# Routed experts of a two-layer trunk: passes counted one by one instead of in pairs

## The reference, cut to what matters

```
s = sigmoid(t @ w_router);  idx = top 4 of (s + b_router);  w = s[idx] / sum(s[idx]) * 2.5
routed = sum over the 4 chosen e of  w_e * (silu(t @ w_e_gate[e]) * (t @ w_e_up[e])) @ w_e_down[e]
shared = (silu(t @ w_s_gate) * (t @ w_s_up)) @ w_s_down
x = x + gate2 * rmsnorm(routed + shared)
```

| layer | tokens of the largest expert of the groups, in order of rank |
|---|---|
| 0 | 176, 121, 109, 84, 69, 59, 48, 37 |
| 1 | 274, 123, 104, 77, 67, 58, 49, 27 |

## Time and profile before

### The profile page before, as it was taken

The page is one execution under the profiler, slowest core; times in us unless marked ns, Lnnn a source line. Parts: engine busy times, 40 slices in busy tenths (PEclk is TensorE's granted clock), DMA queues, the critical chain, the costliest instruction groups (busy, mean ns, idle before and its releaser), DMA issues. The chain is left out here.

```text
span 2462.8 us, 36549 instructions
## 1 busy us (share of the span) xinstructions
PE 2316.8 (94%) x13640; PEld 1420.9 (58%) x13640; DVE 1051.0 (43%) x2010; ACT 636.6 (26%) x1575; POOL 511.7 (21%) x562
## 2 busy tenths in 40 slices
PE   6999999999999999899979999999999999989996
PEld 3656554666577645555455665656656765545552
DVE  3544344643156335322466253546323733452225
ACT  2225201630033022222231350046001501312221
POOL 0213030040224100233221221203012330013331
PEclk8999999999999999999989999999999999999999
DMA  9123465101343021899651226410042312074985
GB/s 327 42 95 103 171 220 177 44 34 60 120 112 89 35 81 40 342 373 398 244 195 69 86 77 253 165 57 1 35 145 104 103 62 72 35 280 184 376 350 229
DMA packets 170192, 368.37 MB, mean 150 GB/s; under 512 B 38836, under 2 KB 52156, under 8 KB 170052
## 3 DMA queue, kind: packets, MB, share of 16 engines
q1 hardware_dynamic: 116400, 259.96, 28.7%
q10 hardware_dynamic: 29972, 56.10, 6.4%
q0 software_dynamic: 23680, 50.43, 6.1%
HBM read 343.99 MB, written 47.56 MB: 159 GB/s over the span
## 5 line engine op out<-in xcount | busy, mean ns | idle before, releaser
L2780 PE MATMUL ps<-ring,mixT 128*32 128x256 f32 x2688 | 215.7, 385 | 1.2 <-DMA ring<-in_w_e_up 1.2
L234 PE MATMUL ps<-ring,hT 128*128 128x512 f32 x480 | 210.3, 595 | 4.8 <-PEq L1401 4.1
L2780 PEld LDWEIGHTS ps<-ring,mixT 128*32 128x32 f32 x2688 | 118.1, 112 | 96.9 <-issue 22.4
L234 PEld LDWEIGHTS ps<-ring,hT 128*128 128x128 f32 x480 | 89.8, 190 | 116.0 <-issue 115.5
L1504 PE MATMUL ps<-late,ring 128*128 128x320 f32 x512 | 145.4, 443 | 3.7 <-PEq L2046 2.5
L2647 PE MATMUL ps<-ring,mixT 128*128 128x512 f32 x320 | 140.5, 598 | 4.4 <-PEq L1401 4.4
L1504 PEld LDWEIGHTS ps<-late,ring 128*128 128x128 f32 x512 | 98.8, 194 | 48.2 <-issue 9.3
L835 PE MATMUL ps<-hT,ring 128*128 128x512 f32 x256 | 114.5, 600 | 2.9 <-ACT ssm_dec L1081 2.9
L2798 PE MATMUL ps<-ring,ex_hidT 128*32 128x512 f32 x768 | 115.4, 598 | 0.7 <-DMA ring<-in_w_e_down 0.7
L412 PE MATMUL ps<-hT,ring 128*128 128x320 f32 x368 | 107.2, 444 | 4.9 <-PEq L1346 2.7
L1467 PE MATMUL ps<-mix_T,mix_S 128*128 128x320 f32 x384 | 107.2, 434 | 3.0 <-DVE mix_part L1590 1.6
(11 more groups left out here) (549 smaller groups left out, 4432.9 us busy)
## 6 DMA issues: line engine op xcount, KB each, us to landing
ring<-in_w_in SPq DMA_DIRECT2D x18, 2048.0 KB, 10.2
ring<-in_w_gate SPq DMA_DIRECT2D x12, 2048.0 KB, 9.8
da_ada_w<-in_w_ada ACTq DMA_DIRECT2D x12, 2048.0 KB, 8.7
ring<-in_w_e_down SPq DMA_DIRECT2D x48, 512.0 KB
ring<-in_w_e_gate SPq DMA_DIRECT2D x40, 512.0 KB
ring<-in_w_e_up SPq DMA_DIRECT2D x40, 512.0 KB
mix_ada_w<-in_w_ada ACTq DMA_DIRECT2D x8, 2048.0 KB, 18.0
ring<-y_rows SPq DMA_DIRECT2D x28, 512.0 KB, 7.9
```

Source lines behind the costliest of these rows:

```text
L234: last = pe.matmul(out, cx.hT[:, k, tok(t)], wide[:, k, :], start=(k == 0), stop=(k == KT - 1))
L2780: ins = pe.matmul(ps[rows, 2 + b, 0:2 * P].rearrange("p (g f) -> p g f", g=2), xT[:, b, k, rows], ew[:, :, k, :], start=(k == 0), stop=(k ...
```

## The change

A group now takes passes one by one: its count is that of its largest expert's sets of 32 tokens, rounded up, and at least 2. The total is rounded up to an even number, in the last group, since ScalarE, VectorE and GpSimd still loop over two passes at a time; TensorE loops over one. `xT`, `hid`, `hidT` and the PSUM banks of `up` (2), `turn_hidden` (3) and `down` (4, 5) are now single. A new buffer `xs` is fixed: VectorE copies the gathered rows from `xg` into it (`stage_rows`), and `turn` reads `xs`. `gather(n)` waits for the copy of pass n-2 and no longer for its transposes. TensorE's order is `up(i) down(i-1) turn(i+1) turn_hidden(i)`, with the first pass of each group written out ahead of the loop. A few VectorE steps of one column each prepare and compute the counts. The core of the diff:

```diff
 LANES = 4
 GRAIN = P // LANES
 GROUPS = NE // LANES
 STRIDE = 3
 N_CHOICE = TOP_K * TILES
...
         before = old[:, 4 * D + TOP_K * TILES * NE:4 * D + (TOP_K + 1) * TILES * NE].rearrange("p (t e) -> p t e", t=TILES)
         xg = old[:, 0:2 * D].rearrange("p (b d) -> p b d", b=2)
-        xT = old[:, 2 * D:4 * D].rearrange("p (b k s) -> p b k s", b=2, k=KT)
+        xs = old[:, 2 * D:3 * D]
+        xT = old[:, 3 * D:4 * D].rearrange("p (k s) -> p k s", k=KT)
...
-                    pool.wait_ge(sem("x_turned"), at(n - 1, i))
-                pool.tensor_copy(index[:, b:b + 1], m.table[:, bass.ds(at(n, i), 1)] if n >= 4 else m.table[:, n:n + 1]).then_inc(
+                    pool.wait_ge(sem("x_staged"), at(n - 1, j))
...
-            def turn(n, i=0):
-                b = n % 2
-                pe.wait_ge(sem(f"xg_ready{b}"), i * (16 * UNROLL // 2) + 16 * (n // 2 + 1))
-                if n:
-
-                    pe.wait_ge(sem("xT_low"), at(n, i))
-                    pe.wait_ge(sem("xT_high"), at(n, i))
+            def turn(n):
+
+                pe.wait_ge(sem("x_staged"), n + 1)
                 for k in range(KT):
-                    ins = pe.transpose(ps[:, k // 4, (k % 4) * P:(k % 4 + 1) * P], xg[:, b, k * P:(k + 1) * P],
-                                       cx.ident)
+                    ins = pe.transpose(ps[:, k // 4, (k % 4) * P:(k % 4 + 1) * P], xs[:, k * P:(k + 1) * P], cx.ident)
                 ins.then_inc(sem("x_turned"), 1)
...
             pe.wait_ge(sem("shared_hid"), 1)
             turn(0)
-            turn(1)
             pe.wait_ge(sem("experts_known"), 1)
             pe.wait_ge(sem("shared_hid"), 2)
             first = 0
             for s in range(GROUPS):
-                last = turns(pe, s)
+                last = passes(pe, s)
                 pe.wait_ge(sem(f"up_full{s % 2}"), 2 * LANES * 16 * (s // 2 + 1))
-                with pe.Fori(first, last) as i:
-                    up(0, i, s)
-                    up(1, i, s)
-                    turn_hidden(0, i)
-                    turn(2, i)
-                    pe.wait_ge(sem(f"down_full{s % 2}"), LANES * 16 * (s // 2 + 1))
-                    down(0, i, s)
-                    turn_hidden(1, i)
-                    turn(3, i)
-                    down(1, i, s)
+                up(first, s)
+                if s:
+                    down(first - 1, s - 1)
+                turn(first + 1)
+                turn_hidden(first)
+                pe.wait_ge(sem(f"down_full{s % 2}"), LANES * 16 * (s // 2 + 1))
+                with pe.Fori(first + 1, last) as i:
+                    up(i, s)
+                    down(i - 1, s)
+                    turn(i + 1)
+                    turn_hidden(i)
                 first = last
+            down(last - 1, GROUPS - 1)
...
+            def turned(n, j=0):
+                act.wait_ge(sem("x_turned"), at(n + 1, j))
+                if n:
+
+                    act.wait_ge(sem("tile_up"), at(n, j))
+                act.activation(xT[:, 0:4, :].rearrange("p k s -> p (k s)"), ps[:, 0, :], ACT.Copy).then_inc(
                     sem("xT_low"), 1)
 
...
+            count = half_passes(act)
+            silu_up(0)
+            turned(1)
+            hidden_out(0)
+            silu_up(1)
+            result(0)
+            turned(2)
+            hidden_out(1)
+            with act.Fori(1, count) as j:
+                for n in range(2):
+                    silu_up(n, j)
+                    result(n - 1, j)
+                    turned(n + 1, j)
+                    hidden_out(n, j)
+            result(-1, count)
...
-            whole(t_of, n_of, 1.0 / PER_TURN, (PER_TURN - 1.0) / (2 * PER_TURN))
-            step(dve, dve.tensor_scalar(t_of, t_of, 1.0, None, ALU.max))
+            whole(t_of, n_of, 1.0 / GRAIN, (GRAIN - 1.0) / (2 * GRAIN))
+            step(dve, dve.tensor_scalar(t_of, t_of, 2.0, None, ALU.max))
...
-            dve.tensor_reduce(ids[:, 1:2], pick[:, 0, 1, :], AX.X, ALU.add).then_inc(sem("ids_ready"), 1)
+            step(dve, dve.tensor_reduce(so_far, pick[:, 0, 1, :], AX.X, ALU.add))
+            whole(half, so_far, 0.5, 0.25)
+            step(dve, dve.tensor_scalar(half, half, of_half, None, ALU.mult))
+            dve.scalar_tensor_tensor(out=ids[:, 1:2], in0=so_far, scalar=of_sum, in1=half, op0=ALU.mult,
+                                     op1=ALU.add).then_inc(sem("ids_ready"), 1)
...
+            def stage_rows(n, j=0):
+
+                b = n % 2
+                dve.wait_ge(sem(f"xg_ready{b}"), j * 16 + 16 * (n // 2 + 1))
+                if n:
+                    dve.wait_ge(sem("x_turned"), at(n, j))
+                dve.tensor_copy(xs[:, :], xg[:, b, :]).then_inc(sem("x_staged"), 1)
+
+            def turned(n, j=0):
+                dve.wait_ge(sem("x_turned"), at(n + 1, j))
+                if n:
+                    dve.wait_ge(sem("tile_up"), at(n, j))
+                dve.tensor_copy(xT[:, 4:8, :].rearrange("p k s -> p (k s)"), ps[:, 1, :]).then_inc(
                     sem("xT_high"), 1)
 
...
             dve.wait_ge(sem("experts_known"), 1)
             turned(0)
+            stage_rows(1)
+            count = half_passes(dve)
+            hidden(0)
             turned(1)
-            count = turns(dve, GROUPS - 1)
-            with dve.Fori(0, count) as i:
-                hidden(0, i)
-                hidden(1, i)
-                turned(2, i)
-                result(0, i)
-                turned(3, i)
-                result(1, i)
+            stage_rows(2)
+            hidden(1)
+            result(0)
+            turned(2)
+            stage_rows(3)
+            with dve.Fori(1, count) as j:
+                for n in range(2):
+                    hidden(n, j)
+                    result(n - 1, j)
+                    turned(n + 1, j)
+                    stage_rows(n + 2, j)
+            result(-1, count)
```

More of the change, by code:

```diff
@@ L60 @@
 N_CHOICE = TOP_K * TILES
[L61 to L63 removed]
+MAX_PASSES = 2 * TOK // GRAIN + 2 * GROUPS
+TABLE = MAX_PASSES + 6
 EVEN = 12582912.0
@@ L2513, in stage_tail, with passes, half_passes, at @@
         block = st.enter_context(nc.Block())
[L2515 to L2521, removed]
+        def passes(eng, s):
+            return eng.value_load(m.words[0:1, P + s:P + s + 1], min_val=2 * s + 2, max_val=MAX_PASSES)
+        def half_passes(eng):
+            return eng.value_load(m.words[0:1, P + GROUPS:P + GROUPS + 1], min_val=GROUPS, max_val=MAX_PASSES // 2 + 1)
+        def at(n, j):
+            return j * 2 + n
         @block.sync
@@ L2563, in _ @@
                 if s >= 2:
-                    passed = turns(sp, s - 2)
-                    sp.wait_ge(sem("tile_up"), passed * UNROLL)
+                    passed = passes(sp, s - 2)
+                    sp.wait_ge(sem("tile_up"), passed)
                 for c in range(LANES):
@@ L2627, in _ @@
             gather(3)
[L2628 to L2633, removed]
+            with pool.Fori(0, count) as j:
+                for n in range(2):
+                    gather(n + 4, j)
+                    scatter(n, j)
+            pool.wait_ge(sem("xg_ready1"), count * 16 + 32)
+            pool.wait_ge(sem("xg_ready0"), count * 16 + 32)
             pool.sem_inc(sem("pool_go"), 1)
@@ L2932, in _ @@
             turned(0)
-            turned(1)
             act.wait_ge(sem("table_known"), 1)
@@ L2970, in _ @@
             ins.then_inc(sem("spare_rows"), 1)
+            so_far, half, of_half, of_sum = (tiny[:, n:n + 1] for n in range(4))
+            step(dve, dve.tensor_scalar(of_half, col, float(GROUPS - 1), 2.0, ALU.is_equal, ALU.mult))
+            step(dve, dve.tensor_scalar(of_sum, col, float(GROUPS), None, ALU.is_equal))
+            step(dve, dve.tensor_tensor(of_half, of_half, of_sum, ALU.add))
+            step(dve, dve.tensor_scalar(of_sum, col, float(GROUPS - 1), None, ALU.is_lt))
             finish_mods(cx, dve, 1, mods).then_inc(sem("mods_known"), 1)
@@ L3081, in _ @@
             step(dve, dve.tensor_scalar(tmp, lane, FAR, None, ALU.mult))
-            step(dve, dve.scalar_tensor_tensor(out=begin, in0=begin, scalar=float(PER_TURN), in1=tmp, op0=ALU.mult,
+            step(dve, dve.scalar_tensor_tensor(out=begin, in0=begin, scalar=float(GRAIN), in1=tmp, op0=ALU.mult,
                                                op1=ALU.add))
@@ L3152, in _, with result @@
+            dve.sem_inc(sem("y_low"), 1)
+            dve.sem_inc(sem("y_high"), 1)
+            shared(1)
+            stage_rows(0)
+            def result(n, j=0):
+                b = n % 2
+                dve.wait_ge(sem("tile_down"), at(n + 1, j))
+                dve.wait_ge(sem(f"y_stored{b}"), j * 16 + 16 * ((n + 2) // 2))
+                dve.tensor_copy(y[:, b, SEC:D], ps[:, 5, :]).then_inc(sem("y_high"), 1)
             dve.wait_ge(sem("experts_known"), 1)
             turned(0)
+            stage_rows(1)
```

116 lines of the change are left out of this document (44 added, 72 removed).

## The result

| | before | changed |
|---|---|---|
| median, us | 2465.1 (2455.6 to 2473.7, 4 runs) | 2490.8 (2481.6 to 2499.5, 4 runs) |
| ratio, first comparison | | 1.0118 (95% interval 1.0078 to 1.0158) |
| ratio, second comparison (run e12 below) | | 1.0087 (1.0059 to 1.0115) |
| profiled execution: time; span | 2464.5; 2462.8 | 2489.8; 2487.7 |
| passes in layers 0 and 1 | 28, 32 | 26, 30 |

A forecast was written before the change was run, and what follows sets the result against it. TensorE's own sequence was taken as the bound, with the DMA engines close behind. +20.2 (passes and wait) - 2 (stalls) - 0.4 (ahead of first pass) = +17.8 us, forecast 2477 us; own range 2470 to 2486, 8-in-10 range 2462 to 2495.

The forecast's parts named there:

- The counts: Expert passes of both layers: 28+32 = 60 become 26+30 = 56, four fewer at 6.44 us, -25.8 us.
- rival (e): Expert passes: the schedule gives other totals than computed, each pass 7.26 us; chance small, within the forecast's 0.63.
- The wait added: TensorE ahead of `up`: 0.8 us wait each pass, period 7.26 us; with four passes fewer, +20.2 us.
- (b): TensorE's loop, now turning once a pass: restart dearer than the wait; with 0.3 us, sum +35, 2494 us; chance 0.2.
- (d): TensorE ahead of `up`: the wait is hidden after all, pass stays 6.44 us, -28, 2431 us; chance 0.04.
- The copy to `xs`: VectorE, beside `up`: 0.75 us a copy, costing nothing; a late gather must last over 3 us before TensorE feels it.
- The clock: Expert passes: 0.8 us idle in each, 11%, does not lower the granted clock of 1.00; nothing added.
- rival (a): Pass loop: clock falls, half of each pass's work at the lower level, 179 us more, 2656 us; chance 0.03.
- Stalls by transfers: TensorE's waits in the passes: gathers -3, weights +1; sum between -3 and +2.5, taken at -2 us.
- Rival (c): Layer 0: weights become the bound, stalls grow 4 us at each of two groups; +25, 2484 us; chance 0.1.
- Ahead of the first pass: Before each layer's first `up`: -1.0 for one `turn` fewer, +0.8 for count steps; -0.4 us for both layers.
- The sum: Whole kernel: +17.8 us, 2477 us on the scale of medians; chance of slower by over 1% 0.28.

The follow-up runs named there:

- e12: The changed kernel itself measured again, with more rounds and a second profile: 2486.4 us, ratio 1.0087 to the kernel before.
- e4: The changed kernel loading only half the columns of each expert's matrices from the third group on (other results): 2473.3 us, ratio 1.0062 to the kernel before.
- e1: The changed kernel with TensorE's `turn(i+1)` moved ahead of `down(i-1)`, copies likewise: 2472.9 us, ratio 1.006 to the kernel before.
- e3: The changed kernel with an unused VectorE sum over 3072 columns ahead of each copy to `xs`: 2499.8 us, ratio 1.0146 to the kernel before.
- e11: The kernel before, loading only half the columns of each expert's matrices from the third group on (other results): 2462.0 us, ratio 0.998.
- e2: The changed kernel with each group's count rounded up to even, 28 and 32 passes again: 2506.4 us, ratio 1.0177 to the kernel before.
- e10: e1 with `turn_hidden(i)` moved ahead of `down(i-1)`, so the transposes stand together: 2477.2 us, ratio 1.0049 to the kernel before.
- e9: e10 with the groups in rank order 5 4 3 2 1 0 7 6: 2462.3 us, ratio 0.9987 to the kernel before.

## Why the prediction was right, step by step

**The counts**: 26 and 30, as worked out; rival (e) is out.

**The wait added**: 0.77 us where 0.8 was worked out, a pass of 7.27 where 7.26 was. The slack of VectorE between the result's copy (to 1103.16) and the critical copy (1103.38) was 0.22, as forecast. Undisturbed, 56 such passes are 400.1 us (e4) against 378.9: +21.2 where the sum had +20.2. e1 shows by removal that the wait is the cause. Rivals (b), a dearer restart, and (d), a hidden wait, are excluded by the same rows.

**The copy to `xs`**: 0.68 us for 0.75, at no cost; e3 confirms the slack of over 3 us.

**The clock**: in the window from 1045 to 1170 us of the changed kernel it was granted at 0.99 with 11% of idle time in each pass, so rival (a), half of all the work at the lower level, did not come. The sentence of the Trainium skill on idle pieces between groups of matmuls ("TensorE: Matmul & The Clock Gate", "A second HAM failure mode: psum-queue depth-cycling") is not borne out at pieces of 0.8 us in 7.3. But the clock was not 1.00 throughout, as the prediction had it: behind the idle piece of 2.72 us it stood at 0.50 and made the stall 1.5 us longer. In e1, with pieces of 5.6 and 6.0 us, the mean of the window fell to 0.95. The prediction weighed the clock for the steady pass alone and not for a late weight.

**Stalls by transfers**: the term that was mis-sized. Taken at -2, they came to +1.2 in the first profile and +4.9 in the second. The prediction let 3 us go with the gathers and added 1 for the weights. Waits for gathers did go, but of the stalls before only some 2.3 us were other things than weights (e11), and the weights, 4.4 before, took 7.9 and 11.6: in the first profile 3.4, 1.6 and 0.4 us in layer 0, 1.1, 0.3, 0.8 and 0.4 in layer 1. The +1 was thus +3.5 and +7.2. The same window before and after, with the share of the DMA engines as the last but one number:

```profile
1045.00:1170.00 125.00, 120.97 (x1647) 65.46 (x1643) 31.89 (x57) 31.83 (x76) 46.37 (x76) 1.00 0.99 386
```

```profile
1045.00:1170.00 125.00, 108.83 (x1467) 65.51 (x1460) 36.73 (x66) 26.61 (x66) 41.79 (x65) 0.99 0.99 382
```

The DMA engines had next to nothing to spare before and have as little after; time that TensorE saves in a group they do not have. In layer 0 the second and the fifth group shrank from 4 to 3 passes, and their ends start the loads of the fourth and the seventh, the two that come late. When e2 gives them the pass back, the share in this window is 0.91 and all stalls together fall to 0.5 us. The prediction named this crowding and priced it too low; the lower clock behind a wait it left out. Rival (c) was thus real in kind: it put 8 us more on the weights of layer 0, where the two profiles have 1.0 and 4.6 more than before. And one sign that the prediction itself called wrong did appear: stalls on weights above 5 us a layer, 5.4 and 9.0 in layer 0.

**Ahead of the first pass**: -1.1 in layer 0 where -0.2 was worked out; within the scatter of that stretch (1007 to 1028 over the profiles), so not settled.

**The sum**: +17.8 forecast, +21 and +26 measured between medians (e12, first comparison). The difference is the stalls (3.2 and 6.9 above the term), one microsecond of the pass term, and scatter of stages that were not touched. On the scale of medians the forecast was 2477 us, and 2490.8 came: within the range of 2462 to 2495, but outside the narrower 2470 to 2486 that the ends of the terms gave. 6 of the 13.8 us between forecast and result are the median of the kernel before, which went from 2459.1 to 2465.1 with a fourth run; as differences, +21 and +26 lie within the +11 to +27 of the narrower range as well. The hit rests on the pass term, which gave +21.2 of it; the term of the stalls had even its sign wrong. The chance of "slower by over 1%" was rightly not small: the first comparison has 1.2%, the second 0.9%.

## What to carry to other kernels

Work taken off an engine is worth its time only if nothing is uncovered by it and the next resource has room: here four passes (26 us) were paid with 0.8 us of exposed copy in each of 56, and once the copy was covered again (e1, e10), 21 to 33 us of stalls on late weights took its place. Before saving passes, read the DMA share of the same window: at 0.99 it warned that a shorter group would wait. Price a late transfer by its wait and by the slower products behind it. In a single-buffered pipeline it is the order that covers the copies: ask of every copy which product stands between the step that makes it due and the step that needs it, and choose the order of work units so that the transfers' busy and idle stretches balance.

## What the hardware showed that was not expected

A change on TensorE between transposes over the whole array and products by columns of 32 costs 0.14 to 0.15 us each: with four changes a pass e1 takes 6.73 us, with two e9 and e10 take 6.44, with the same instructions and no idle time in the rows; (6.73 - 6.44) / 2 = 0.145. The kernel before, with four changes in a turn of two passes, takes 6.44 as well.

The granted clock fell behind single idle pieces, and how long it stayed down differed: after a wait of 2.72 us in the changed kernel `up` took 4.93 us instead of 3.45, after one of 5.62 us in e1 6.21 instead of 3.6. After the changed kernel's wait of 2.31 us at layer 0's seventh group `up` took its usual time.

GpSimd's `y_rows` DMA issues took 1180 ns in the mean in the changed kernel against 1078 before. In a steady pass of the changed kernel the issue starts at 1104.45, 0.22 us before VectorE's copy to `xs` ends, and takes 1.12 us; before, with no such copy, 1.02. In e3, where the added sum and not the copy lies beside the issue, it takes 1.03. That the overlap is the cause was not tested further.
